# Twelve of 18 weight units of the second block split and stored during the first projection instead of during the attention

## What is computed

```python
# block 1
hn = rms_norm(h, norm_mix_g)
proj = hn @ w_in                          # 1024 x 3072: 24 units of 128 columns
y_dil = dilated_mixture_attention(...)    # 8 heads of 64, all 1024 keys with a bias
y_na = neighbourhood_attention(...)       # 8 heads of 64, 512 or 640 keys per 128 queries
h = h + concatenate([rms_norm(y_dil), rms_norm(y_na)]) @ w_out    # 8 units
h = h + hierarchical_moe(rms_norm(h), ...)                        # 16 experts
# block 2
h = rmsnorm(x, attn_norm)
q, k, v, g, gk_low, s5_u, rg_x, rg_gate = split(h @ w_in_2)       # 18 units, called in2 here
x = x + concatenate([gla, s5, rglru]) @ w_out_2
x = x + conv_ffn(rmsnorm(x), ...)
```

## Time and profile before

| what | value |
|---|---|
| median of 3 runs | 2463.29 us |
| the three runs | 2463.03, 2463.29, 2469.86 us |
| span of the profiled execution | 2462.7 us (0.6 below the median; a time of its own is not listed) |
| busy: PE, PE weight loads, DVE, ACT, POOL | 94%, 74%, 48%, 24%, 40% |
| chain that ended last | PE 80%, DVE 8%, POOL 4%, DMA 3%, issue 3% |
| moved by DMA | 277 MB, mean 112 GB/s |

### The profile page before, as it was taken

How to read it: one execution, slowest core, us unless ns; L and a number is a source line. 1 busy time by engine, 2 the same in 40 slices (tenths; PEclk the granted TensorE clock), 3 DMA queues, 4 the chain that set the end, 5 groups by cost and what they waited for, 6 DMA issues and landing times.

```text
span 2462.7 us, 28863 instructions
## 1 busy us (share of the span) xinstructions
PE 2302.7 (94%) x11232; PEld 1814.8 (74%) x11232; DVE 1173.0 (48%) x1895; ACT 591.2 (24%) x831; POOL 982.5 (40%) x600
## 2 busy tenths in 40 slices
PE   7999999998989399999689999899999999999997
PEld 6888799997877266666466556678888888888875
DVE  7996444444632322222478877755432243233135
ACT  3100266566641211111131004222110011011011
POOL 2333554565632665810302872224233332332324
PEclk9999999999999799999899999899999999999998
DMA  4231253334541777932632221211111111111103
GB/s 155 78 120 69 68 185 120 118 125 154 176 162 52 274 292 287 349 126 81 252 120 103 79 92 51 102 36 51 44 44 42 60 46 41 60 47 37 63 26 112
DMA packets 89908, 277.01 MB, mean 112 GB/s; under 512 B 6896, under 2 KB 38768, under 8 KB 82608
## 3 DMA queue, kind: packets, MB, share of 16 engines
q1 hardware_dynamic: 71120, 188.84, 21.7%
q0 software_dynamic: 8576, 45.42, 5.0%
q10 hardware_dynamic: 10080, 40.90, 4.3%
HBM read 198.59 MB, written 76.55 MB: 112 GB/s over the span
## 4 chain that ended last, share of the span: by engine, by line
PE 80%; DVE 8%; POOL 4%; DMA 3%; issue 3%; ACT 2%; SPq 0%; DVEq 0%; POOLq 0%; ACTq 0%
PE ps L869 15%; PE ps L871 15%; PE ps L873 15%; PE ps L991 6%; PE ps L1088 4%; PE ps L968 3%; PE ps L977 3%; PE ps L1072 2%; PE ps L1068 2%; PE ps L1070 2%; PE ps L1069 2%; PE ps L851 1%; PE ps L854 1%; PE ps L853 1%; PE ps L1056 1%
## 5 line engine op out<-in xcount | busy, mean ns | idle before, releaser
L869 PE MATMUL ps<-work_part 128*128 128x512 f32 x1760 | 548.0, 393 | 2.8 <-DVE work L2363 1.7
L873 PE MATMUL ps<-work_part 128*128 128x512 f32 x1760 | 542.4, 389 | 0.0
L647 POOL CAST work_part<-ring 128x1024 fp32r<-128x1024 f32 (+2 forms) x124 | 118.6, 956 | 784.3 <-PE ps L873 659.7
L869 PEld LDWEIGHTS ps<-work_part 128*128 128x128 f32 x1760 | 329.9, 188 | 77.3 <-issue 6.8
L873 PEld LDWEIGHTS ps<-work_part 128*128 128x128 f32 x1760 | 330.7, 188 | 69.2
L871 PE MATMUL ps<-work_part 128*128 128x512 f32 x1152 | 354.6, 389 | 0.0
L651 POOL TENSOR_TENSOR work_part<-ring,work_part 128x1024 fp32r<-128x1024 f32 (+2 forms) x124 | 281.4, 2269 | 15.9 <-PE ps L1286 6.1
L871 PEld LDWEIGHTS ps<-work_part 128*128 128x128 f32 x1152 | 216.2, 188 | 44.9
L991 PE MATMUL ps<-work,hT 128*128 128x64 f32 x1600 | 196.2, 273 | 2.5 <-ACT hT L1417 2.5
L991 PEld LDWEIGHTS ps<-work,hT 128*128 128x128 f32 x1600 | 190.4, 193 | 4.5 <-ACT hT L1417 2.3
L871 PE MATMUL ps<-hT_part,work_part 128*128 128x512 f32 x608 | 188.0, 391 | 0.0
(11 more groups left out here) (374 smaller groups left out, 3506.1 us busy)
## 6 DMA issues: line engine op xcount, KB each, us to landing
pages<-w_moe SPq DMA_DIRECT2D x16, 2048.0 KB, 9.5
ring<-w_up_units SPq DMA_DIRECT2D x44, 512.0 KB, 3.2
ring<-w_in_units SPq DMA_DIRECT2D x42, 512.0 KB, 3.7
w_parts<-work_part SPq DMA_DIRECT2D x36, 512.0 KB, 3.5
work_part<-w_parts SPq DMA_DIRECT2D x36, 512.0 KB, 4.0
pages<-w_moe SPq DMA_DIRECT2D x16, 1024.0 KB, 6.4
x_slots<-hT SPq DMA_DIRECT2D x31, 512.0 KB, 5.2
work<-x_slots ACTq DMA_DIRECT2D x31, 512.0 KB, 5.9
```

What stands on the lines that cost most here:

```text
L647: pool.tensor_copy(WHI[n % 2][:, 0:cols], w).then_inc(whi_ready, 1)
L869: pe.matmul(ps[:, c], whi[:, w], hi[k][:, c], start=(k == 0), stop=False)
L873: mm = pe.matmul(ps[:, c], wlo[:, w], hi[k][:, c], start=False, stop=(k == len(hi) - 1))
```

## The change

A constant `EARLY = 12`. The in2 units 0 to 11 are now handled during the first projection, 12 to 17 during heads 1 to 6 of the attention.

- POOL: `split_in2(n-1)` right behind `split(n)`, for n from 1 to 12. In the attention `split_in2(12)` to `(17)` follow heads 1 to 6; heads 0 and 7 to 15 have none, and the two behind head 15 are gone.
- Buffers: the raw early units land in pages 12 and 14 of `work`, and are split in place, high part to page 13 or 15 and low part to page 12 or 14. `n_mix`'s third scratch page moves from 15 to 11. ACT, before it writes the results 12 and 14 into these pages, waits until the parks are done.
- SP: raw units 0 and 1 are loaded behind raw unit 4 of the first projection. From u = 6 on, each turn of SP's loop issues the load of raw unit u, then the two parks of in2 unit u-6, and from u = 7 on then a wait for the parks of unit u-7 and the load of in2 unit u-5.
- In the attention the stores of zeros no longer alternate with 18 parks; six parks are done between them.
- Some semaphores are joined (`x_again` and `cst_again` into `reloaded`, four of the routing into `route_diff` and `route_exp`), to free numbers.

```diff
-        parts_order = list(range(0, U_OUT)) + list(range(U_IN2, U_OUT2)) + list(range(U_OUT, U_IN2)) + list(range(U_OUT2, len(units)))
+        parts_order = [0]
+        for u in range(1, U_OUT):
+            parts_order += [u] + ([U_IN2 + u - 1] if u <= EARLY else [])
+        parts_order += list(range(U_IN2 + EARLY, U_OUT2)) + list(range(U_OUT, U_IN2)) + list(range(U_OUT2, len(units)))
...
+        EARLY_RAW = [Wp[12], Wp[14]]
+
+        def in2_split(n):
+
+            if n < EARLY:
+                return Wr[13 + 2 * (n % 2)][:, :], Wr[12 + 2 * (n % 2)][:, :]
+            return Wr[38][:, :], Wr[37][:, :]
...
             def load_in2(n):
-                sp.dma_start(ring[:, 0, :], units[U_IN2 + n]).then_inc(w_loaded[0], 16)
+                if n < EARLY:
+                    sp.dma_start(EARLY_RAW[n % 2], units[U_IN2 + n]).then_inc(early_loaded[n % 2], 16)
+                else:
+                    sp.dma_start(ring[:, 0, :], units[U_IN2 + n]).then_inc(w_loaded[0], 16)
 
             def park_in2(n):
+                hi, lo = in2_split(n)
                 sp.wait_ge(wlo_ready, order_of[U_IN2 + n] + 1)
-                sp.dma_start(w2_parts[n, 0], Wr[38][:, :].bitcast(f32)).then_inc(parked, 16)
-                sp.dma_start(w2_parts[n, 1], Wr[37][:, :].bitcast(f32)).then_inc(parked, 16)
-                sp.wait_ge(parked, 32 * (n + 1))
-                if n + 1 < 18:
-                    load_in2(n + 1)
+                sent = early_parked[n % 2] if n < EARLY else parked
+                sp.dma_start(w2_parts[n, 0], hi.bitcast(f32)).then_inc(sent, 16)
+                sp.dma_start(w2_parts[n, 1], lo.bitcast(f32)).then_inc(sent, 16)
...
+                if u == 4:
+                    load_in2(0)
+                    load_in2(1)
+                if 6 <= u < EARLY + 6:
+                    park_in2(u - 6)
+                if 7 <= u < EARLY + 5:
+                    n = u - 5
+                    sp.wait_ge(early_parked[n % 2], 32 * (n // 2))
+                    load_in2(n)
...
             for n in range(24):
                 split(n)
+                if 1 <= n <= EARLY:
+                    split_in2(n - 1)
...
-                split_in2(h)
-            split_in2(16)
-            split_in2(17)
+                if 1 <= h <= 18 - EARLY:
+                    split_in2(EARLY + h - 1)
...
+                if m in (12, 14):
+                    act.wait_ge(early_parked[(m - 12) // 2], 32 * (EARLY // 2))
```

More of the change, by code:

```diff
@@ L26 @@
 KSPLIT = 6
+EARLY = 12
 FF = 22
@@ L135, in build @@
         x_loaded = [sem(f"x_loaded{i}") for i in range(4)]
+        early_loaded = [sem(f"early_loaded{i}") for i in range(2)]
+        early_parked = [sem(f"early_parked{i}") for i in range(2)]
         cst_loaded = sem("cst_loaded")
         strip_loaded = [sem(f"strip_loaded{i}") for i in range(2)]
-        x_again = sem("x_again")
         s5_loaded = sem("s5_loaded")
@@ L228, in build @@
         for u in parts_order:
+            if U_IN2 <= u < U_IN2 + EARLY:
+                continue
             at_ring = 0 if in2(u) else ring_at(u)
@@ L301, in build @@
         U_QKV += [take(1) for m in range(2, 7)]
-        n_mix = add_late_norm(Hp, "norm_mix", [Wp[22], Wp[23], Wp[15]], mix_use, take(1), (BHI, [hTr[t][:, :] for t in range(NT)]))
+        n_mix = add_late_norm(Hp, "norm_mix", [Wp[22], Wp[23], Wp[11]], mix_use, take(1), (BHI, [hTr[t][:, :] for t in range(NT)]))
         U_QKV += [take(1) for m in range(7, 16)]
@@ L441, in build @@
         emptied[P_LOGIT] = (logit_ready, 1)
-        emptied[P_ROUTE], emptied[P_RANK] = (gdiff_ready, 1), (rank_read, 1)
+        emptied[P_ROUTE], emptied[P_RANK] = (route_diff, 1), (rank_read, 1)
         for b in range(NBLK):
@@ L590, in _ @@
                     sp.wait_ge(wlo_ready, order_of[U_OUT - 3] + 1)
-                    load_in2(0)
+                    load_in2(EARLY)
                     sp.wait_ge(zero_set, 1)
-                    for n in range(U_OUT2 - U_IN2):
-                        park_in2(n)
-                        for b in range(2 * n, min(2 * n + 2, NBLK)):
-                            if b >= 4:
-                                sp.wait_ge(scores_ready, NU // (NBLK + 1) * (b - 3))
-                            sp.dma_start(x_slots[b * P:(b + 1) * P, :].rearrange("p (k n) -> p k n", n=P), ZERO.unsqueeze(1).to_broadcast([P, NT, P])).then_inc(slots_zeroed, 16)
+                    for b in range(NBLK):
+                        if b >= 4:
+                            sp.wait_ge(scores_ready, NU // (NBLK + 1) * (b - 3))
+                        sp.dma_start(x_slots[b * P:(b + 1) * P, :].rearrange("p (k n) -> p k n", n=P), ZERO.unsqueeze(1).to_broadcast([P, NT, P])).then_inc(slots_zeroed, 16)
+                        n = EARLY + (b - 5) // 2
+                        if b % 2 == 1 and EARLY <= n < 18:
+                            park_in2(n)
+                            if n + 1 < 18:
+                                sp.wait_ge(parked, 32 * (n + 1 - EARLY))
+                                load_in2(n + 1)
                 if u == U_OUT + 2:
@@ L655, in split_in2 @@
                 u = U_IN2 + n
-                hi, lo = Wr[38][:, :], Wr[37][:, :]
-                pool.wait_ge(w_loaded[0], raw_loads[u])
-                if n >= 1:
-                    pool.wait_ge(parked, 32 * n)
-                pool.tensor_copy(hi, ring[:, 0, :]).then_inc(whi_ready, 1)
+                hi, lo = in2_split(n)
+                if n < EARLY:
+                    raw = EARLY_RAW[n % 2]
+                    pool.wait_ge(early_loaded[n % 2], 16 * (n // 2 + 1))
+                    if n >= 2:
+                        pool.wait_ge(early_parked[n % 2], 32 * (n // 2))
+                else:
+                    raw = ring[:, 0, :]
+                    pool.wait_ge(w_loaded[0], raw_loads[u])
+                    if n > EARLY:
+                        pool.wait_ge(parked, 32 * (n - EARLY))
+                pool.tensor_copy(hi, raw).then_inc(whi_ready, 1)
                 pool.wait_ge(whi_ready, order_of[u] + 1)
-                pool.tensor_tensor(lo, ring[:, 0, :], hi.bitcast(f32), ALU.subtract).then_inc(wlo_ready, 1)
+                pool.tensor_tensor(lo, raw, hi.bitcast(f32), ALU.subtract).then_inc(wlo_ready, 1)
                 pool.wait_ge(wlo_ready, order_of[u] + 1)
@@ L1148, in _ @@
                 if c == 0:
[L1149 removed]
+                    pe.wait_ge(reloaded, 32)
                 for gate in range(2):
```

32 lines of the change are left out of this document (15 added, 17 removed).

## The result

| | median | lowest to highest | runs |
|---|---|---|---|
| before | 2465.69 us | 2463.03 to 2469.86 | 4 |
| changed | 2507.72 us | 2506.35 to 2512.01 | 4 |

The ratio is 1.0178, with a 95% interval of 1.0161 to 1.0194: the change makes the kernel slower by 42.0 us. 2491.7 was forecast, so the direction is right, and 42.0 stands against 28.4 in size. The median lies at the very top of the range of 2467 to 2508, outside the 2480 to 2501 of the forecast's own case. The profiled execution's span went from 2462.7 to 2505.4.

The account below looks back on a forecast made before the run. PE was taken to bound the kernel. Loop 32.9 + clock 2 - attention's end 4.5 - DVE beside POOL 2 = 28.4 on the profiled 2462.7, with the median 0.6 above: 2491.7 us, range 2467 to 2508.

Parts of the forecast that it names:

- the forecast's own case: Projection: a closed loop with L from 6.8 to 8.9, total 2480 to 2501 us, chance 0.74.
- What bounds the kernel: Whole kernel: PE, busy 7 to 9 tenths in nearly every slice; other engines' work matters only where PE waits.
- The closed loop: First projection: split(n), four DMAs, in2 split n-1, split(n+1), L + 7.1 us a turn; PE starts unit 13 32.9 us later.
- the size of L: Projection: time from the first of four DMAs to the last landing, taken as 8.0 us, ends 5.0 and 9.5.
- L of 9.5 in all turns: Rival in the projection: the batch is slower, L about 9.5 or more, 2506.7 us, chance 0.10.
- The rule of 6.8 us: Projection's DMA batch: fixed 2.0 us plus bytes at 436 GB/s, 6.8 us for 2.1 MB, a loop of 13.9.
- PE's clock: Behind the projection's last gap: half speed for up to some 7 us, costing 0 to 3.5, taken as 2 us.
- End of the attention: Output projection: split(24) runs earlier, but PE stands again for the scaled rows; 4.5 us won, ends 0 and 8.6.
- DVE beside POOL, 2 us won: Attention heads 7 to 15: one meeting of DVE with a POOL subtraction goes; 2 us won, 0 to 4.
- Costed at nothing: Projection and attention: ACT's two new waits, joined semaphores, the zeros and DVE's turn tables cost nothing.
- The load that doesn't queue: Rival in the projection: L about 5.0, loss 2.9 against gain 6.5, 2459.7 us, chance 0.10.
- DVE as the bound: Rival in the projection: with a quick loop, twelve in2 splits hold DVE's turn tables, 2.1 us each, 2474.3 us, chance 0.06.

Follow-up runs that it names:

- the second profile: The changed kernel run and profiled once more, with nothing altered: 2507.81 us.
- the load ahead: Changed kernel with the in2 unit's load moved to the head of SP's turn, before the wait for the split: 2492.57 us, 1.0111 of before.
- the short-split kernel: As the load ahead, but the twelve early in2 splits work on one column instead of 1024 and the raw page is parked twice: 2459.89 us, 0.9982.
- two splits behind some heads: Kernel before, with no in2 split in the projection and two behind heads 2, 4 and 6 of the attention: 2459.25 us, 0.9983.
- the loop with short splits: Changed kernel, SP queue as it is, with the twelve early in2 splits on one column and the raw page parked twice: 2472.12 us, 1.0035.

## Why the prediction was right or wrong

*What bounds the kernel*: right. Before, PE waits 1.3 us in the projection and 8.6 at the attention's end, and what the change puts in PE's way in the projection is paid for.

*The closed loop*: right in mechanism, in place (units 5 to 13) and in form (L + 7.1 a turn); **the term that failed is the size of L, put at 8.0 in every turn**. Measured: seven turns of 8.0 to 8.2, three of 9.4, 9.8 and 10.2, with the gaps between SP, DMA and POOL 8.7 a turn. Ten turns of 0.7 more are 7.2 us. A further 0.9 comes from the first turn, which I costed as starting at 39.0 as before: in2 split 0 ran beside DVE's wide work on `hT_part` (its CAST took 3.32 us instead of 1.04), PE waited 1.7 us for `hT_part` where it hadn't before, and `split(2)` began at 36.43, not 35.45. Together the loop is 41.0 instead of 32.9. Of the 14.3 us between the 28.4 forecast and the 42.7 of the profiled execution these are 8.1; 2.1 are the attention (below), 0.4 the smaller gain at its end, 0.1 the clock and 3.6 the stages behind. I had the long turns as a case of its own (L of 9.5 in all turns, 2506.7, chance 0.10) and never as a mixture, though rows on either side of 8.0 were before me. That the measured 2507.7 is near that case is chance: its loop was 47.9, with gains of 6.5 against it. The mean of 8.7 is what four loads took in the earlier trace rows, and I had taken 0.7 off for the stores being lighter. In seven turns of ten that held; what it left out is that a batch has a second length.

*The rule of 6.8 us* doesn't hold for this batch. No wait for a raw unit was under 7.8 us in the kernels that keep the load last. The Trainium skill (DMA: Bandwidth & Descriptors, the anatomy of one DMA) gives a fixed 2.0 us and 436 GB/s, fitted for one DMA on GpSimd's path; carried over to this batch on SP's queue that is an estimate of 6.8 us, and the traces do not agree.

*PE's clock*: right, 2 forecast, 2.1 measured.

*End of the attention*: right, 4.5 forecast, 4.1 and 4.0 measured here, 3.9 to 5.0 in the other runs, with the wait on the scaled rows taking the other half, 4.12, as described.

*DVE beside POOL, 2 us won*: right by itself. PE's wait of 1.89 at 625.94 is gone. The attention as a whole took 0.1 us more than before in one profile and 2.6 in the other, because of the next term; in the second profile it also ran 17.1 us at 1.2 GHz instead of 10.2.

*Costed at nothing*: this failed for the zeros. I looked at when they are wanted and not at what they run beside; four stores at once delay the first bias strip, and the attention's first step takes 3.1 us more. That is read from the traces of the two orders; no run moves the zeros alone. It held for ACT's waits and the joined semaphores. The turn tables were late (last store at 234.1 instead of 205.3), under cover of a PE that was later.

*The rivals.* The load that doesn't queue fell: it queues. DVE as the bound was given 0.06, for a quick loop only, and that condition was right: it shows as soon as the loop is open. Its price and place were wrong: I took 2.1 us for each split and the turn tables as the first consumer, 2474.3 in all. The kernels with the load ahead show 3.6 to 4.4 us for each. I had also counted it against this rival that DVE's instructions are narrow, and narrow ones are held as long as wide ones. The first consumer is the inverse norm, made at 86.8 and wanted at 96.8, which I had not looked up; with the loop opened it was 2492.57. Had L come out at 5, the case that I priced at 2459.7 would have been far off, since DVE lay under it. The Trainium skill (SBUF — State Buffer, who interferes with whom) has the port of DVE and GpSimd locked for a whole instruction; here the trace agrees: 2.2 us against 0.17, with ends 0.02 us from those of POOL's subtractions.

*What is left.* 3.6 us of the profiled execution lie in stages that the change leaves alone. They are 2.0 in the second profile, and one profile of the short-split kernel, 2472.45 beside its median of 2459.89, had 9 of that kind. The low clock takes its part in such differences. But all twelve other profiles have between 1.3 and 9.3 there against the one profile of the kernel before, also that of two splits behind some heads; with a single profile of before, a lucky execution and a small real loss can't be told apart, and the cause stays open.

## What to carry to other kernels

Before moving work into a stage, draw the loop that it makes: if the load of the next unit is asked for only after the instruction that stands right ahead of its user, the whole latency of the batch is paid each time, and an average share of idle DMA says nothing of it. Then look under that bound for the next: an engine whose chain of small dependent instructions is held by the one that gets the new work is slowed by about as much as the other works (2.8 to 4.4 us for a split of 3.5 here), however small its instructions are. When a queue's work is moved away, look at what now goes out earlier behind it, and beside which transfer: here it was the zeros. And where a gain is only "nothing left at the end", look first for idle time in the stage itself: the two splits behind a head cost nothing there.

## What the runs showed of the hardware

**A narrow instruction of DVE is held as long as a wide one of POOL.** 128x8 instructions went from 0.17 to 2.2 us beside a 128x1024 subtraction. The kernel before has such meetings with the projection's own splits; there they fell on TENSOR_SCALARs (L1779, 28 of 128x8, mean 303 ns, with the load ahead 455). By form, for DVE from 30 to 86 us (busy, mean ns of one, idle before), before and with the load ahead:

```profile
L1784 DVE TENSOR_TENSOR small<-small 128x8 f32<-128x8 f32 x36 | 6.0, 167 | 1.2
```

```profile
L1824 DVE TENSOR_TENSOR small<-small 128x8 f32<-128x8 f32 x36 | 21.8, 604 | 1.2
```

**Batches of the same four DMAs take 8 or 10 us, at the same places each time.** The long turn at 62.20 of the changed kernel, GB/s in 40 slices of 61 to 73 us and its DMAs (KB, us to landing):

```profile
GB/s 0 0 0 0 0 0 0 137 82 218 205 137 177 314 410 355 382 423 437 396 410 423 410 423 437 410 410 219 82 27 27 27 27 14 27 0 0 0 0 0
...
q8 instruction: 1, 0.02, 0.5%
...
work<-w_in_units SPq DMA_DIRECT2D x1, 512.0 KB, 8.4
```

and a short one, 78 to 88 us:

```profile
GB/s 0 0 0 0 0 0 0 0 33 115 115 262 262 262 229 229 213 426 393 442 426 377 459 393 442 426 377 459 426 410 426 393 311 82 33 0 0 0 0 0
...
work<-w_in_units SPq DMA_DIRECT2D x1, 512.0 KB, 6.8
```

Both run at some 420 GB/s; the long one ends with 1.8 us at 27 or less, which is 420 / 16: the rate of one of the 16 DMA engines, so it looks as if one finished alone. In each of the three long turns a queue named "instruction" (q8) moved 0.02 MB, as in one of the seven short ones; in the loop with short splits, two of three long turns had it. The places repeat: the second, seventh and tenth turn in both profiles of the changed kernel. Whether loading code is what holds that engine wasn't tried, and stays open.
